# Dilated attention: biases added by VectorE instead of by products with a reversing matrix, the reversal moved into the queries' and outputs' turns, and blocks of unread products removed

## The reference

```python
DIL_GROUPS = ((128, 1), (512, 4), (2048, 16))
...
        mask, bias = band_mask_and_bias(window, dil, qb.shape[2], rel_bias[:, hs])
        logits = jnp.einsum('brnqhd,brnkhd->brnhqk', qb, kw).astype(jnp.float32) * scale
        logits = jnp.where(mask[:, None], logits + bias, NEG_INF)
        m = jnp.max(logits, axis=-1, keepdims=True)
        p = jnp.exp(logits - m)
        l = jnp.sum(p, axis=-1, keepdims=True)
        o = jnp.einsum('brnhqk,brnkhd->brnqhd', p, vw) / jnp.swapaxes(l, 3, 4)
```

## Time and profile before

| | us |
|---|---|
| median of 3 runs | 2259.11 |
| range of these runs | 2256.03 to 2265.84 |
| the profiled execution's own time | 2271.0 |
| span of its trace | 2269.2 |

### The profile page before, as it was taken

How to read it: one execution, slowest core, us unless ns; L and a number is a source line. 1 busy time by engine, 2 the same in 40 slices (tenths; PEclk the granted TensorE clock), 3 DMA queues, 4 the chain that set the end, 5 groups by cost and what they waited for, 6 DMA issues and landing times.

```text
span 2269.2 us, 33265 instructions
## 1 busy us (share of the span) xinstructions
PE 2169.4 (96%) x14214; PEld 1782.5 (79%) x14214; DVE 1408.1 (62%) x1456; ACT 1030.6 (45%) x1155; POOL 80.5 (4%) x138
## 2 busy tenths in 40 slices
PE   6999899999999899999999999889999999999999
PEld 4777777688787777778788897777888888887887
DVE  5767744689775744499765655466556675635664
ACT  4344322467545422377644545335445444535443
POOL 2040000000000000000000000000000000020000
PEclk9998899999999899999999998999999999999999
DMA  9863879999660858999555550006555556433553
GB/s 346 329 224 110 292 252 371 366 336 367 207 241 7 275 205 307 331 344 368 186 186 188 167 182 1 4 11 215 186 186 166 195 172 204 147 95 120 195 186 112
DMA packets 267314, 475.62 MB, mean 210 GB/s; under 512 B 9424, under 2 KB 151824, under 8 KB 262944
## 3 DMA queue, kind: packets, MB, share of 16 engines
q1 hardware_dynamic: 256128, 431.81, 54.8%
q0 software_dynamic: 11040, 41.70, 5.5%
HBM read 471.33 MB, written 2.14 MB: 209 GB/s over the span
## 4 chain that ended last, share of the span: by engine, by line
PE 85%; DVE 7%; ACT 4%; DMA 3%; issue 2%; SPq 0%; ACTq 0%; DVEq 0%
PE psum L1069 14%; PE psum L1071 7%; PE psum L1086 3%; PE psum L1088 3%; PE psum L1087 3%; PE psum L1037 3%; PE psum L1038 3%; PE psum L1039 3%; PE psum L1406 3%; PE psum L1361 2%; PE psum L1362 2%; PE psum L1363 2%; PE psum L1518 2%; PE psum L1520 2%; PE psum L1519 2%; DVE w_lo L2798 2%
## 5 line engine op out<-in xcount | busy, mean ns | idle before, releaser
L2798 DVE TENSOR_TENSOR w_lo<-ring,w_hi 128x2048 fp32r<-128x2048 f32 x267 | 609.9, 2289 | 290.8 <-ACT w_hi L2149 284.8
L2149 ACT ACTIVATE w_hi<-ring 128x2048 fp32r<-128x2048 f32 x267 | 510.8, 1915 | 363.9 <-PE psum L1088 119.8
L1069 PE MATMUL psum<-h_both,w_hi 128*128 128x512 f32 x1408 | 499.7, 399 | 1.7 <-DVE h_both L3492 1.3
L1071 PE MATMUL psum<-h_both,w_lo 128*128 128x256 f32 x1408 | 395.3, 281 | 0.0
L1069 PEld LDWEIGHTS psum<-h_both,w_hi 128*128 128x128 f32 x1408 | 264.5, 188 | 68.4 <-issue 1.7
L1071 PEld LDWEIGHTS psum<-h_both,w_lo 128*128 128x128 f32 x1408 | 265.9, 189 | 1.4
L2798 DVE TENSOR_TENSOR w_lo<-pool,w_hi 128x2048 fp32r<-128x2048 f32 x70 | 160.4, 2291 | 107.5 <-ACT w_hi L2149 107.1
L2149 ACT ACTIVATE w_hi<-pool 128x2048 fp32r<-128x2048 f32 x70 | 134.1, 1916 | 163.9 <-DMA pool<-in_exp_w_up 59.2
L2171 ACT ACTIVATE pool<-psum 128x512 f32<-128x512 f32 x88 | 52.6, 598 | 261.5 <-PE psum L1071 261.5
L1037 PE MATMUL psum<-w_hi,h_both 128*128 128x512 f32 (+1 forms) x352 | 141.8, 403 | 6.6 <-DVE w_lo L2798 4.4
L1361 PE MATMUL psum<-h_both,w_hi 128*128 128x256 f32 x480 | 139.1, 290 | 0.6 <-DVE w_lo L2798 0.6
(11 more groups left out here) (476 smaller groups left out, 3813.2 us busy)
## 6 DMA issues: line engine op xcount, KB each, us to landing
ring<-in_ffn_pre_w_in SPq DMA_DIRECT2D x44, 1024.0 KB, 5.1
ring<-in_ffn_post_w_in SPq DMA_DIRECT2D x44, 1024.0 KB, 5.1
pool<-in_exp_w_up SPq DMA_DIRECT2D x40, 1024.0 KB, 7.9
ring<-in_exp_w_gate SPq DMA_DIRECT2D x36, 1024.0 KB, 7.6
ring<-in_exp_w_down SPq DMA_DIRECT2D x30, 1024.0 KB, 7.6
ring<-in_ada_w SPq DMA_DIRECT2D x24, 1024.0 KB, 7.1
ring<-in_ffn_pre_w_out SPq DMA_DIRECT2D x22, 1024.0 KB, 4.9
ring<-in_ffn_post_w_out SPq DMA_DIRECT2D x22, 1024.0 KB, 4.9
```

What stands on the lines that cost most here:

```text
L1069: pe.matmul(o.rearrange("p (s n) -> p s n", s=2), wh[:, k, fs], h_both[:, :, k, :], start=k == 0, stop=False, skip_group_check=True)
L1071: m = pe.matmul(o[:, 0:T], wl[:, k, fs], h_hi[:, k, :], start=False, stop=k == KD - 1, skip_group_check=True)
L2149: act.activation(w_hi[:, (s["split"] + r) % 3, :], piece(s["pieces"][r]), ACT.Copy)\
L2798: dve.tensor_tensor(w_lo[:, slot, :], piece(s["pieces"][r]), w_hi[:, slot, :].bitcast(F32), ALU.subtract).then_inc(sem("w_lo"), 1)
```

## The change

It does four things. (1) The job's bias is `None` for TensorE, so L1123 no longer runs in stage `dil`; VectorE adds the bias tiles to the scores, out of PSUM into the buffer of probabilities, reduces from there, and ScalarE's exponential reads and writes that buffer in place. (2) The bias tiles have reversed queries, so queries are reversed too: their turn is a product with `anti` instead of a transpose for blocks 0 to 2 of `dil_q`, and block 0 of `b_mix` reverses the outputs back in the same way. (3) `anti` is loaded ahead of the 24 bias tiles on GpSimd's queue instead of behind them, and the wait for it is at `dil_q`. (4) The calls of `warm` outside `attention` go: 4 + 6 + 3 + 4 + 6 + 4 + (3 + 7) + 18 + 4 + 3 = 62 products. Those inside `attention` stay.

```diff
+        def biases_dil(h, t):
+            return view(WORK, 3, 1536)[:, :, 384 * h + P * t:384 * h + P * t + P * (t + 1)]
...
-                                 bias=bias_dil(g, h, t),
+                                 bias=None,
...
+            pl.dma_start(anti, a["c_anti"]).then_inc(sem("mem_in"), 16)
             for g in range(3):
                 for h in range(4):
                     for t in range(NT):
                         toeplitz(bias_dil(g, h, t), 8 + 4 * g + h, t).then_inc(sem("bias_in"), 16)
-            pl.dma_start(anti, a["c_anti"]).then_inc(sem("bias_in"), 16)
...
+                        elif nm == "dil_q" and i < 3:
+                            m = pe.matmul(o, src, anti, start=True, stop=True)
...
+                        if nm == "b_mix" and b == 0:
+                            m = pe.matmul(bank(at)[:, P * k:P * k + P], xn[:, t, P * j:P * j + P], anti, start=True, stop=True)
...
             pe.wait_ge(sem("keep_in"), 32)
-            warm(4, 6)
             norm("n_mem")
...
             pe.wait_ge(sem("ret_moved"), 2)
-            warm(6, 4)
...
-            warm(3, 4)
             gemm("even_out", beside_out)
...
-            warm(4, pair_of("a_in", 3))
...
-            warm(6, 2)
             pe.wait_ge(sem("rw_sig"), 2)
             pe.wait_ge(sem("rw_gate"), 2)
             key_norms(range(6))
...
             transposes("mem0_q", ("heads_ok", 3))
-            warm(4, 2)
             transposed("mem0_q")
...
             for t in range(NT):
-                warm(7 if t else 3, 6)
                 pe.wait_ge(sem("rw_out"), t + 1)
...
             gemm("b_q")
-            warm(18, 4)
-            transposes("dil_q", ("heads_ok", 5))
-            warm(4, 0)
+            transposes("dil_q", ("heads_ok", 5), ("mem_in", 64))
             transposed("dil_q")
-            attention("mem1", ("mem_in", 48))
-            attention("dil", ("bias_in", 272 + 25 * 16))
+            attention("mem1")
+            attention("dil")
             mix_blocks("b_mix", ("att_o", 24), ("att_o", 24))
-            warm(3, 4)
             gemm("b_out")
...
-                        src, segs = logits(j, groups), len(groups[0])
-                        dst = probs[j % 2]
+                        dst, segs = probs[j % 2], len(groups[0])
+                        src = dst[:, 0:segs, 0:n] if kind == "dil" else logits(j, groups)
...
+                        src = logits(j, groups)
+                        if kind == "dil":
+                            if j == 0:
+                                dve.wait_ge(sem("bias_in"), 272 + 24 * 16)
+                            dve.wait_ge(sem("att_pt"), J - 1)
+                            biased = probs_of(kind)[0][j % 2][:, 0:3, 0:groups[0][0]["n"]]
+                            step(dve.tensor_tensor(biased, src, biases_dil(*jobs[j][1:]), ALU.add))
+                            src = biased
```

More of the change, by code:

```diff
@@ L962, in mix_blocks @@
                         j, t = 2 * b + k // 2, k % 2
-                        m = pe.transpose(bank(at)[:, P * k:P * k + P], xn[:, t, P * j:P * j + P], ident)
+                        if nm == "b_mix" and b == 0:
+                            m = pe.matmul(bank(at)[:, P * k:P * k + P], xn[:, t, P * j:P * j + P], anti, start=True, stop=True)
+                        else:
+                            m = pe.transpose(bank(at)[:, P * k:P * k + P], xn[:, t, P * j:P * j + P], ident)
                     m.then_inc(sem("mix_ps"), 1)
@@ L2778, in attention @@
                             dve.wait_ge(sem("att_exp"), J - 1)
-                        dve.tensor_reduce(nmax[:, j % 2, 0:len(groups)], logits(j, groups), AX.X if len(groups) == 2 else AX.XY,
+                        src = logits(j, groups)
[6 more added lines that the diff above has]
+                            src = biased
+                        dve.tensor_reduce(nmax[:, j % 2, 0:len(groups)], src, AX.X if len(groups) == 2 else AX.XY,
                                           ALU.max, negate=True).then_inc(sem("att_logits"), 1)
```

## The result

The changed kernel takes 2274.57 us, median of six runs (2272.2 to 2278.09), against 2261.92 for six runs of the kernel before on the same chips (2256.03 to 2265.84). The ratio is 1.0055 [1.0042, 1.0069], +12.65 us: **slower**, inside what the rival "stage dil itself loses the clock" gave (2270 to 2279) and just above the range of the prediction. By the difference, +12.65, it is near that rival's lower figure of +11. The profiled execution took 2273.49 us, with a span of 2271.7 and a mean granted clock of 0.969 (0.981 before).

A forecast was written before the change was run, and what follows sets the result against it. TensorE was taken as the bound, in stage dil replaced by the loop through VectorE and ScalarE. Terms of -5.3 us without the clock and +8.5 for it gave +3.2: 2262 us from the median of 2259.11, range 2252 to 2274.

The forecast's parts named there:

- stage dil itself loses the clock: Rival: TensorE's idle time in stage dil drops its clock; +13 instead of -3.5, total +20 at most, 2270 to 2279; chance 0.17.
- the term for stage `dil`: Stage dil without bias products: a pair takes 6.5 us instead of 7.61, 0.9 comes back at the end; -3.5 us.
- ate none of it, so that rival: Rival: in stage dil VectorE's additions lie fully on the path, so nothing is gained there; +3.5, 2266; chance 0.1.
- +1.5 for the products: At dil_q: twelve transposes become products, 0.245 us each instead of 0.12, on the path to mem1's scores; +1.5 us.
- -0.9 for the block: Behind dil_q: the removed unread products stood between VectorE's last copy and the scores; -0.9 us.
- +2.5 for the clock: Ahead of dil_q: after a 7.93 us gap the turns start at half clock; one and a half stretches at 1.64 us.
- -3.5 for the three in the way: Unread products that delay later work: ahead of att -1.0, ahead of mem0 -1.6, behind dil_q -0.9 us.
- +8.5 for the clock: Half clock at the start, dil_q, key norms with mem0, and b_out: 5.2 stretches at 1.64 us, +8.5 us.
- my "nothing": At a_out: the clock falls earlier, but a wait behind the first weight piece goes; no cost counted.

## Why the prediction was wrong

- **The step that failed** is the term for stage `dil`, -3.5 us. It priced the stage at full clock throughout; measured, the stage is 41.5 - 32.9 = 8.6 us longer, because TensorE ran 34 us of it at half clock.
- **Why I took that step** is the weighing of the rival "stage dil itself loses the clock", 0.17. I argued against it that "pieces as long stand in all attention stages without it, and 5.45 of 6.5 us is a far denser load than the 1.40 of 3.40". The kernel with only the start filled shows the second half wrong: the loop at 6.4 to 6.9 us a pair lost its clock 19 us in, and one product more in each turn kept it. The first half is contradicted by the trace of before itself. In its stage `att` a wait of 1.43 us, in the last turns, is followed by half clock, and part of `mem0` runs at half clock too, although `mem0` has unread products between its turns:

```profile
177.37 0.66 PE L1142 MATMUL psum<-pool 128*128 128x64 f32 x4 [1.43 <-ACT pool L2211]
```

```profile
178.00:184.00 6.00, 6.00 (x28) 5.45 (x27) 3.37 (x7) 5.09 (x5) 0.00 (x0) 0.50 0.80 298
1396.50:1406.70 10.20, 10.20 (x38) 7.91 (x38) 5.28 (x8) 6.20 (x13) 0.00 (x0) 0.50 0.00 0
```

- **What I didn't look at** is the start of the stage. The bias products were also what TensorE did while the first reductions and exponentials ran. With them gone it waits 0.77 and 1.42 us in the first two turns, and there the clock fell. I followed the loop in its steady state only.
- **The price of that rival was right by the pair and too high for the stage.** A pair at half clock measures 10.58 us where twice the work gave 10.9. The rival charged +13 for four such pairs and +20 in all; the stage measures +8.6, since its first 5 us or so still ran at full clock, and the medians give +12.65.
- **The stage at full clock was right**: 6.50 us a pair in the filled kernels (6.5 foreseen), 32.9 - 28.9 = 4.0 us saved (3.5 foreseen). The additions took 0.96 and 0.56 us and ate none of it, so that rival is excluded.
- **The turns were right**: +3.3 us to `mem1`'s scores (6.9 against 3.6), where +1.5 for the products, -0.9 for the block and +2.5 for the clock made +3.1. At full clock, with the block of 18 back, the twelve products take 2.94 us in three kernels of the experiments, as in the earlier trace rows. With stage `dil` this makes 11.9 of the 12.65 us.
- **The removed blocks**: alone they measure +2.3 to +3.5 us, with no change inside the interval; my terms, -3.5 for the three in the way and +8.5 for the clock, made +5. The three in the way give 2.7 back (3.5 foreseen), which isn't clear of noise. Two of them in the changed kernel's timeline of all engines, ahead of `att` and of `mem0`:

```profile
156.16 1.13 DVE L2786 TENSOR_REDUCE tiny<-psum 128x2 f32<-128x256 f32 x2
...
1386.23 2.43 DVE L3396 SCALAR_TENSOR_TENSOR pool<-pool,rcols,psum 128x256 f32<-128x256 f32 x6
...
1388.88 2.08 PE L1134 MATMUL psum<-pool 64*128 64x256 f32 x8 [1.90 <-issue]
```

  The first is 1.2 us earlier than in the earlier trace rows; the scores start 0.2 us behind VectorE's 1388.66, where the block had ended 1.7 us behind 1387.54. Half clock at `dil_q` and at `a_out` does follow the blocks: the seven traces without the blocks at these two places have 7 to 14 us of it at `dil_q` and 10 at `a_out`, the five with them none at `dil_q` and at most 7 at `a_out`. At `a_out` it costs nothing that can be seen, which bears out my "nothing": from the end of `mem0` to the turns of `dil_q` the seven take 589.8 to 591.6 us, the five 590.7 to 597.9. What the clock costs at the other places outside stage `dil` isn't shown, as single stretches come and go between executions of one kernel.
- **The median** of before was 2259.11 in the three runs that I had and 2261.92 in six: about 3 us of my distance are in that.

The chain, as shown: the bias products gone from stage `dil` → TensorE idle 0.77 and 1.42 us in its first turns → half clock for 34 us → pair 10.58 instead of 6.5. Where the start is filled, a wait of 0.89 us in each pair is left, and the clock falls later. Filling both undoes it; the blocks outside aren't needed for it.

One thing is not separated. The bias products, and the unread products that replace them, shorten the waits and also change what kinds of work TensorE has. The length of a wait alone doesn't decide: with 64-row products the stage has a wait of 1.22 us in its last turns and keeps its clock. No run here lengthens or shortens the waits with the work unchanged.

## What to carry to other kernels

Work that is taken off the bounding TensorE may be what keeps its clock. Price the stage at 1.2 GHz as well, and take the change with its replacement: a product whose result nobody reads, in each idle piece, the first turns of a loop included. While another engine sets the pace, such a product costs nothing (a pair takes 6.50 us with it and 6.57 without). Look at the granted clock in stretches, not at busy shares: here a stage had 98% busy TensorE and ran at half speed. An unread product that ends behind the mark that its successor waits for is in the way, and is the first candidate to go; the 2.7 us for three such blocks are a hint of that and no proof.

## What the hardware showed that I had not expected

- In the 34 us at half clock TensorE was on record as busy for 33.29 us, and the clock came back only in the stage's last turns. In the run with one block it came back earlier, behind six unread products in a row (5.22 us).
- In stage `dil` filled at its start, the clock fell within a stretch that has TensorE busy for 17.26 of 19 us; filled throughout with 64-row products it stayed, with 26.37 of 29. Over these stretches the two shares are the same, 0.91, so the share over a stage doesn't tell whether it keeps its clock. The first has waits of 0.89 us in its loop, the second none above 0.36 there.
- One kernel can have two heaps of times some 12 us apart (loop filled, start not); its profiled execution has the same waits of 0.77 and 1.42 us in the first turns as the changed kernel.
